# A ring of four half buffers for the features of a trunk's two output stages

## The reference, cut to what matters

```python
y_lat = (mixed features, 2048 per token) @ w_out          # ev_w_out in layer 0, od_w_out in layer 1
h_lat = layer_norm(DEEPNORM_ALPHA * h_lat + g_l * y_lat, ln_g[layer], ln_b[layer])
```

## Time and profile before

| | us |
|---|---|
| median of 3 runs | 3099.26 |
| all three runs | 3095.19, 3099.26, 4453.72 |
| the profiled execution, its own time | 3095.66 |
| its span, first to last instruction | 3093.9 |
| mean granted TensorE clock | 0.971 of 2.4 GHz |
| PE busy | 2925.7 (95% of the span) |
| DVE, ACT, POOL busy | 1545.2, 1181.3, 145.2 |

### The profile page before, as it was taken

The page is one execution under the profiler, slowest core; times in us unless marked ns, Lnnn a source line. Parts: engine busy times, 40 slices in busy tenths (PEclk is TensorE's granted clock), DMA queues, the critical chain, the costliest instruction groups (busy, mean ns, idle before and its releaser), DMA issues. The chain is left out here.

```text
span 3093.9 us, 38194 instructions
## 1 busy us (share of the span) xinstructions
PE 2925.7 (95%) x15623; PEld 2508.3 (81%) x15623; DVE 1545.2 (50%) x2605; ACT 1181.3 (38%) x1957; POOL 145.2 (5%) x205
## 2 busy tenths in 40 slices
PE   7999999999999999969979997999999999998798
PEld 7788888888888888857867886888888888887577
DVE  2625652654355536453533224666656656564353
ACT  2313322331233123322233213666666666665310
POOL 0100000000000000002310000000000000000000
PEclk8899999999999999989989998999999999999899
DMA  6311131113111311163341221100000100100432
GB/s 185 95 27 46 45 113 30 43 52 106 30 52 43 113 31 43 33 221 102 123 136 38 96 89 39 32 25 28 25 28 22 36 21 29 36 14 18 174 109 68
DMA packets 223863, 200.77 MB, mean 65 GB/s; under 512 B 12141, under 2 KB 194301, under 8 KB 223690
## 3 DMA queue, kind: packets, MB, share of 16 engines
q1 hardware_dynamic: 207194, 171.28, 18.3%
q0 software_dynamic: 4656, 16.56, 1.4%
q10 hardware_dynamic: 11840, 10.49, 1.0%
HBM read 157.34 MB, written 40.95 MB: 64 GB/s over the span
## 5 line engine op out<-in xcount | busy, mean ns | idle before, releaser
L40 PE MATMUL v_pj<-e_u_hi,e_w_hi 128*128 128x512 f32 (+1 forms) x864 | 309.3, 358 | 1.9 <-PEq L57 1.9
L40 PE MATMUL v_pj<-e_u_hi,v_w_hi 128*128 128x512 f32 (+1 forms) x864 | 309.1, 358 | 0.0
L41 PE MATMUL v_pj<-e_u_lo,e_w_hi 128*128 128x512 f32 (+1 forms) x864 | 307.4, 356 | 0.0
L41 PE MATMUL v_pj<-e_u_lo,v_w_hi 128*128 128x512 f32 (+1 forms) x864 | 307.4, 356 | 0.0
L42 PE MATMUL v_pj<-e_u_hi,e_w_lo 128*128 128x512 f32 (+1 forms) x864 | 307.2, 356 | 0.0
L42 PE MATMUL v_pj<-e_u_hi,v_w_lo 128*128 128x512 f32 (+1 forms) x864 | 306.9, 355 | 0.0
L40 PE MATMUL o_y_bank<-o_w_hi,o_m_hi 128*128 128x512 f32 x576 | 230.8, 401 | 49.4 <-DVE o_w_lo L1218 30.3
L1816 ACT CAST t_pt_hi<-t_ring 128x512 fp32r<-128x512 f32 (+1 forms) x384 | 181.2, 516 | 251.1 <-PE t_ring L1999 251.1
L1914 DVE TENSOR_REDUCE t_bias<-t_scores 128x1 f32<-128x1280 f32 x128 | 190.6, 1489 | 77.1 <-PE t_scores L2025 76.4
L41 PE MATMUL o_y_bank<-o_w_lo,o_m_hi 128*128 128x512 f32 x576 | 229.0, 398 | 0.0
L42 PE MATMUL o_y_bank<-o_w_hi,o_m_lo 128*128 128x512 f32 x576 | 228.3, 396 | 0.0
(11 more groups left out here) (374 smaller groups left out, 6324.0 us busy)
## 6 DMA issues: line engine op xcount, KB each, us to landing
e_w_raw<-in_ev_w_in SPq DMA_DIRECT2D x72, 512.0 KB, 4.7
v_mw<-in_mod_w SPq DMA_DIRECT2D x32, 512.0 KB, 4.0
l_w_raw<-in_od_w_in SPq DMA_DIRECT2D x21, 512.0 KB, 3.9
o_m_raw<-mixT SPq DMA_DIRECT2D x20, 512.0 KB, 5.4
m_w<-in_mod_w SPq DMA_DIRECT2D x16, 512.0 KB, 7.8
o_w_raw<-in_ev_w_out SPq DMA_DIRECT2D x16, 512.0 KB, 10.4
zgT<-l_lat_q POOLq DMA_DIRECT2D x16, 512.0 KB, 3.5
t_zg<-zgT SPq DMA_DIRECT2D x32, 256.0 KB, 2.7
```

Source lines behind the costliest of these rows:

```text
L40: nc.tensor.matmul(out, whi, xhi, start=first, stop=False)
L41: nc.tensor.matmul(out, whi, xlo, start=False, stop=False)
```

## The change

The two whole-tile buffers become a ring of four half buffers, each with a semaphore of its own for its loads. `HALVES` fixes the order in which halves take slots: (0,0), (1,0), (0,1), (1,1), then (2,0), (2,1), (3,0), ... So tiles 0 and 1 put their first halves into slots 0 and 1 and their second halves into slots 2 and 3; tile 2 takes slots 0 and 1, tile 3 slots 2 and 3, and so on. `first_pair` signals a new semaphore, `first_half`, when PE is through the first eight k of both tiles. SP's two loads of tile 2 are moved ahead of its loop and wait for that signal; its splits on ACT and DVE are moved ahead of their loops, so on DVE ahead of `norm(0)`. In all three loops the loads and splits of tile n + 2 become those of tile n + 3, at the same place of iteration n. The load of tile n still waits for the end of tile n - 2 on PE (for tile 3: tile 1, as before).

```diff
-    YB = 3
+    YB, SLOTS = 3, 4
+    HALVES = [(0, 0), (1, 0), (0, 1), (1, 1)] + [(n, h) for n in range(2, count) for h in range(2)]
+    order_of = numbered(HALVES)
+    slot = lambda n, h: (order_of[(n, h)] - 1) % SLOTS
...
             def load_m(n, h):
-                b = n % 2
-                if n >= 2:
-                    sp.wait_ge(y_half, half_at[(n - 2, 1)])
-                sp.dma_start(m_raw[b][:, half(h), :], src[:, half(h), n * P:n * P + P]).then_inc(m_in[b][h], 16)
+                b = slot(n, h)
+                if n == 2:
+                    sp.wait_ge(first_half, 1)
+                if n > 2:
+                    sp.wait_ge(y_half, half_at[(max(n - 2, 1), 1)])
+                sp.dma_start(m_raw[b][:, :, :], src[:, H * h:H * h + H, n * P:n * P + P]).then_inc(m_in[b], 16)
...
             load_res(1)
+            load_m(2, 0)
+            load_m(2, 1)
             for n in range(count):
+                if n + 3 < count:
+                    load_m(n + 3, 0)
+                    load_m(n + 3, 1)
                 if n + 2 < count:
-                    load_m(n + 2, 0)
-                    load_m(n + 2, 1)
                     load_res(n + 2)
...
+            split(2, 0)
+            split(2, 1)
             for n in range(count):
-                if n + 2 < count:
-                    split(n + 2, 0)
-                    split(n + 2, 1)
+                if n + 3 < count:
+                    split(n + 3, 0)
+                    split(n + 3, 1)
                 if layer == 0:
                     modulate(n)
...
             for n in range(count):
                 norm(n)
-                if n + 2 < count:
-                    split(n + 2, 0)
-                    split(n + 2, 1)
+                if n + 3 < count:
+                    split(n + 3, 0)
+                    split(n + 3, 1)
...
             def products(n, k, o, m_waits=None):
-                b = n % 2
+                b, i = slot(n, k // H), k % H
...
+                    if k == H - 1:
+                        last.then_inc(first_half, 1)
```

More of the change, by code:

```diff
@@ L1057, in stage_out @@
         m_hi, m_lo, m_raw = [], [], []
-        for b in range(2):
-            m_hi.append(s.sb(f"m_hi{b}", [P, KM, P], F32R))
+        for b in range(SLOTS):
+            m_hi.append(s.sb(f"m_hi{b}", [P, H, P], F32R))
             m_at = next_offset(nc)
-            m_lo.append(s.sb(f"m_lo{b}", [P, KM, P], F32R))
-            m_raw.append(over(nc, f"o{layer}_m_raw{b}", [P, KM, P], F32, m_at))
+            m_lo.append(s.sb(f"m_lo{b}", [P, H, P], F32R))
+            m_raw.append(over(nc, f"o{layer}_m_raw{b}", [P, H, P], F32, m_at))
         res = [s.sb(f"res{b}", [P, D]) for b in range(2)]
@@ L1074, in stage_out @@
         w_in = [s.sem(f"w_in{k}") for k in range(KM)]
-        m_in = [[s.sem(f"m_in{b}{h}") for h in range(2)] for b in range(2)]
+        m_in = [s.sem(f"m_in{b}") for b in range(SLOTS)]
+        first_half = s.sem("first_half")
         res_in = [s.sem(f"res_in{b}") for b in range(2)]
@@ L1085, in stage_out @@
         cols = lambda o: slice(512 * o, 512 * o + 512)
-        half = lambda h: slice(H * h, H * h + H)
         @block.sync
@@ L1163, in split @@
             def split(n, h):
-                b = n % 2
-                act.wait_ge(m_in[b][h], 16 * (n // 2 + 1))
-                nc.scalar.copy(m_hi[b][:, half(h), :], m_raw[b][:, half(h), :]).then_inc(m_hi_ok, 1)
+                b = slot(n, h)
+                act.wait_ge(m_in[b], 16 * ((order_of[(n, h)] - 1) // SLOTS + 1))
+                nc.scalar.copy(m_hi[b][:, :, :], m_raw[b][:, :, :]).then_inc(m_hi_ok, 1)
             def split_w(k):
@@ L1208, in _ @@
         def _(dve):
-            split_no = iter(range(1, 2 * count + 1))
             def split(n, h):
-                b = n % 2
-                dve.wait_ge(m_hi_ok, next(split_no))
-                nc.vector.tensor_tensor(m_lo[b][:, half(h), :], m_raw[b][:, half(h), :], f(m_hi[b][:, half(h), :]), ALU.subtract).then_inc(m_ok, 1)
+                b = slot(n, h)
+                dve.wait_ge(m_hi_ok, order_of[(n, h)])
+                nc.vector.tensor_tensor(m_lo[b][:, :, :], m_raw[b][:, :, :], f(m_hi[b][:, :, :]), ALU.subtract).then_inc(m_ok, 1)
             def split_w(k):
@@ L1276, in products @@
             def products(n, k, o, m_waits=None):
-                b = n % 2
-                return mm3(nc, y_bank[n % YB][:, cols(o)], (m_hi[b][:, k, :], m_lo[b][:, k, :]), (w_hi[:, k, cols(o)], w_lo[:, k, cols(o)]),
+                b, i = slot(n, k // H), k % H
+                return mm3(nc, y_bank[n % YB][:, cols(o)], (m_hi[b][:, i, :], m_lo[b][:, i, :]), (w_hi[:, k, cols(o)], w_lo[:, k, cols(o)]),
                            k == 0, k == KM - 1)
@@ L1286, in first_pair @@
                         if k % H == 0:
-                            pe.wait_ge(m_ok, 2 * (k // H) + n + 1)
+                            pe.wait_ge(m_ok, order_of[(n, k // H)])
                         for o in range(2):
@@ L1298, in project @@
                         if o == 0 and k % H == 0:
-                            pe.wait_ge(m_ok, half_at[(n, k // H)])
+                            pe.wait_ge(m_ok, order_of[(n, k // H)])
                         last = products(n, k, o)
```

## The result

Median 3073.3 us (3072.32 to 3075.05, five runs), against 3099.26 before in the same session: ratio 0.9921, 95% interval 0.9906 to 0.9935. The ratio is made from all the fast runs and is not the quotient of the two medians (0.9916); the one run of before that took 4453.72 us is outside it. The forecast was 3074.5 within 3069 to 3085. The profiled execution took 3072.58 us with a span of 3070.8; all rows of after come from it.

A forecast was written before the change was run, and what follows sets the result against it. PE, busy in 95% of the span, was taken as the bound. Stops ahead of tile 2 (17.49 us) and tile 3 (2.49 + 2.31) sum to 22.3 us: 3073.4, plus 1.1 for run scatter, gives 3074.5 us, range 3069 to 3085.

The forecast's parts named there:

- Layer 0, tile 2, 8.25 us: PE's stop between first pair and tile 2 in layer 0 goes: 5.75 us of pause, 2.50 of slow matmuls.
- Layer 0, tile 3, 4.80 us: PE's stop behind the transposes of tiles 0 and 1 goes: 2.49 us of pause, 2.31 of slow matmuls.
- Layer 1, 9.24 us: PE's stop between first pair and tile 2 in layer 1 goes: 7.53 us of pause, 1.71 of slow matmuls.
- both moves as one term: Moving tile 2's load and splits earlier removes the stops ahead of tile 2 in both layers: 17.49 us together.
- norm(n) behind the split: On DVE norm(n) ends 14.5 us behind tile n, 8.2 us to spare before layer 0's transposes; cost 0.
- Rival 2: Layer 0, transposes of tile 1: norm(1) 2 us late after a 14.1 us landing, clock falls; 3078.8 us, chance 0.08.
- Rival 1: Layer 0: clock still falls behind the transposes, so only 20.0 us go; 3076.8 us, chance 0.20.
- Rival 4: Layer 0, tiles 2 to 7: norm(n) too late for its transposes, six stops, 44 us; 3118 us, chance 0.03.
- POOL and DVE: POOL's multiplications start behind the norm, not ahead of the split, so DVE's splits should return to 1.25 us each.
- the 1.1 us that I added: Added to 3073.4 us because the runs shown lie between 0.5 below and 3.6 above the profiled execution.

The follow-up runs named there:

- act_order_only: Kernel before, with only ACT's order changed: it splits tile n + 3 ahead of modulate(n), tile 2 ahead of its loop; 3092.85 us, ratio 0.9982.
- experiments 3 and 4: Changed kernel with DVE splitting tile 2 only behind norm(0) (3093.48 us), and changed kernel with tile 2's load issued as late as before (3092.29 us).
- Experiments 5 and 6: Changed kernel with 8 (3072.0 us, one run) or 16 (3079.36 us) extra statistics operations on DVE in norm(2) to norm(7) of layer 0.
- late_load_early_split: Changed kernel, but SP issues tile 2's load only when tile 0 is through PE, the split staying ahead of norm(0); 3092.29 us, 0.9981 of the kernel before.
- norm_plus_16_stats: Changed kernel with 16 extra statistics operations on DVE in each of norm(2) to norm(7) of layer 0; 3079.36 us, 0.9949 of the kernel before.
- signal_at_14th: Changed kernel with the signal for tile 2's load after the contraction's 14th piece instead of the 8th; 3078.64 us, 0.9950 of the kernel before.

## Why the prediction was right, point by point

- *Layer 0, tile 2, 8.25 us.* From the end of the pair to the end of tile 2: 1410.91 - 1380.85 = 30.06 before, 1396.15 - 1374.39 = 21.76 after: 8.30.
- *Layer 0, tile 3, 4.80 us.* From there to the end of tile 3: 30.91 before, 1422.10 - 1396.15 = 25.95 after: 4.96. A matmul can start 0.41 us behind the start of the last row of transposes, not 0.66, the modelled duration that I had added, so the pause was 0.25 us longer than I reckoned; what the slow matmuls took back made 0.09 less. act_order_only shows this term alone, with 4.98.
- *Layer 1, 9.24 us.* From the end of the pair to the last L40: 139.2 before, 3060.2 - 2930.3 = 129.9 after: 9.3. The stage's other 0.4 us are in its first pair: the wait for tile 1's features there was 9.9 - 7.4 = 2.5 us before and 1.6 after, and slightly more slow matmuls took part of that back.
- *Both parts needed.* I had put layer 0's stop down to the load first and layer 1's to DVE's order, and priced both moves as one term without saying that in each stage either of them alone holds tile 2; experiments 3 and 4 show that it does. Had only one been made, the same sum would have been wrong by 17 us by the terms, and by about 18 as measured.
- *norm(n) behind the split.* Predicted to end 14.5 us behind its tile with 8.2 to spare; norm(3) ended at 1436.44, 14.34 behind 1422.10, and 8.33 before 1444.77. Experiments 5 and 6 bracket it: 8 operations fit, and 16 are late by 1.2 us. Rival 2 did not come either: norm(1) ended at 1388.76, 7.4 us before tile 2 did, where I had 7.
- *Rival 1, the clock,* was no rival but a coin beside the forecast. In nine profiles tile 3 starts right behind the transposes of tile 1. In six it runs at full clock from end of tile to end of tile in 25.9 to 26.0 us; in late_load_early_split, norm_plus_16_stats and signal_at_14th it takes 27.5. The windows of signal_at_14th, whose tile 3 starts at 1406.94:
```profile
1406.00:1407.00 1.00, 0.48 (x5) 0.48 (x5) 0.00 (x0) 0.47 (x2) 0.00 (x0) 1.00 1.16 331
1407.00:1408.00 1.00, 1.00 (x5) 0.81 (x4) 0.00 (x0) 0.87 (x1) 0.00 (x0) 0.53 1.22 312
```
  The clock went to 1.2 GHz just as the dense work began again. Its price was 1.6 us, not 2.3, and three in nine is more than my 0.20, though so few can't tell the two apart. The Trainium skill (TensorE: Matmul & The Clock Gate, Part 1: The HAM clock gate) has the gate judge on a clock of its own; that equal pauses end in both ways agrees with it.
- *Rival 4's price was wrong in its form.* I had six stops; there are stops at every second tile only, so the same lateness costs half. To be slower than before, a stop would have had to be twice as long as I wrote (22.3 / 3 = 7.4 us); that is an estimate, no run had stops so long.
- *POOL and DVE.* POOL's gain now comes behind the norm, as predicted, and no split meets it: DVE's L1222 took 1224 to 1229 ns in all 36 cases, where it had reached 3421 before, and DVE is busy 1527.2 us instead of 1545.2. POOL's bias operation fell from 3.25 to 2.39 us. None of this is on the path. The Trainium skill (SBUF — State Buffer, SBUF: two separate sides) has a VectorE operation with two SBUF inputs and a GpSimd one that reads SBUF block each other. That each is short again where they no longer meet agrees with it, and so does: DVE's second split ended at 1447.28 + 5.79 = 1453.07, 1.09 us behind POOL's bias operation (1448.73 + 3.25 = 1451.98), as if it had waited for it.
- *The size of the whole.* 22.3 us forecast; the medians differ by 26.0 in the first session and by 22.5 in the later one, the profiles' stages by 23.0. The terms are right by their rows; that the median came within 1.2 us of 3074.5 is in part luck, since the stretches without any code of the change moved by 6.4 and -6.3 us between the two profiles, and since the 1.1 us that I added rests on how two runs lay.

## What to carry to other kernels

Where an engine waits at a hand-over, list everything that ends near the moment of release, not only the releaser that the profile names: in layer 1 the load with its cast and the normalization ahead of the split ended about 2 us apart, and taking out one of them gave 0.3 or 1.9 us, where both gave 9.7. Price a stop with the slow matmuls behind it, and measure it by the length of the touched stage in the trace, or better from tile to tile in it: the untouched parts scatter by 6 us from one execution to the next, and a stage's first pair by up to 1.9, mostly with the moment at which the clock rises in it. When a chain of tiles turns late, check whether a stop gives the next tile its time back before multiplying it by the number of tiles.

## What the runs showed that I had not expected

- Three row loads of 512 KB at a stage's start, first needed more than 50 us later, together cost as much as one of the larger stops that this change removed: moving them gave 11.8 us in the medians, 8.3 of it in rows of the two stages, against 8.3 and 9.3 for the stops ahead of tile 2.
- None of the three stops of 1.1 to 1.3 us ahead of the transposes in norm_plus_16_stats let the clock fall, while the thin stretch around tile 1's transposes, 4.1 us with sixteen transposes in it, did so in three profiles of nine.
